# A hybrid decoder step on one core: the samples' and the prompt's softmaxes spread over the stick-breaking unit steps, and cache values in two passes

## The chip, the cores and the metric

One core of one Trainium2 chip runs the whole kernel. The metric is the device time of one execution in microseconds, the median of three runs.

## The reference

One layer of a decoder step, all in f32, for a prompt of 512 tokens and 8 samples with one new token each and 2048 cached positions in 16 pages of 128:

```python
h = rmsnorm(x, g_attn); z = h @ w_in            # 2840 columns
# stick-breaking heads (8), z = q k / 8, mask: key before query
log_1m = where(mask, log_sigmoid(-z), 0)
after  = reverse_cumsum(log_1m) - log_1m
o_sb   = where(mask, exp(log_sigmoid(z) + after), 0) @ v
# NSA heads (8 in 2 groups): compressed, selected (16 of 33 blocks), window
p_c = softmax(q kc); imp = sum over the group of p_c @ overlap; idx = top_k(imp, 16)
o_n = g0 * p_c vc + g1 * softmax(q k[idx]) v[idx] + g2 * softmax(window) v
x = x + [rmsnorm(o_sb), rmsnorm(o_n)] @ w_out
x = x + relu(rmsnorm(x) @ w_up)**2 @ w_down;  y = rmsnorm(x, g_final)
```

In the prompt all 8 selection blocks are within the 16 chosen, so the selected branch is plain causal attention; the block choice is computed for the samples alone. The caches are read by page id: keys and values of the stick-breaking cache (256 KB a page for each), of the selection cache (64 KB a page for each), the compression cache, and a window buffer.

## The kernel before

Each engine has one program in program order, joined by semaphores; `Chain` makes an instruction wait for the one before it on its own engine. SP issues the loads, one after the other. The stages in order of time are: input projection, loading and scoring of the cached keys with compression (until about 463 us), the prologue of the softmaxes, the unit steps, the output projection and the feed-forward part.

**Prologue** (462 to 534 us). PE (lines 807 to 877) and DVE (1729 to 1822) take turns, ACT fills in: `cp_qk`, `cp_max`, `cp_exp`, `cp_soft`, `cp_tr`, `cp_pT` are the prompt's compressed softmax, for four query tiles i, through banks 4 to 7 and `pbuf`; `row_max`, `row_max_diagonal`, `row_max_over`, `row_max_subtract`, `samples_exp`, `row_sum`, `row_sum_over`, `row_reciprocal` are the samples' window (0) and selected (1) softmaxes; `c_s` to `c_selm` the block choice (`rankA`, `rankB` compare 33 importances pairwise, in 1089 columns); `s_abs`, `s_sp`, `s_suf`, `s_c`, `s_d`, `s_a` the samples' stick-breaking logs, with `suf` summed over later pages by 15 chained additions.

**Unit steps** s = 0 to 47. Steps 0 to 15 are stick-breaking units m (head pair `pr`, key tile i = 3, 2, 1, 0, columns n = 128, 256, 384, 512, for two heads): `sb_qk` (PE), `sb_ln` (ACT, abs, exp, ln), `sb_soft` (DVE, three passes: sum, its rounded high part, its rounded low part), `sb_sum` (PE, high and low parts against `ntri` and `nones`, rounded matmuls), `sb_exp` (ACT), `sb_pv` (PE, two steps late). They use bank pairs 2 * (m % 3), so `sb_qk(m)` waits for the exponential of m - 3. Steps 16 to 47 are NSA units n = s - 16: `n_qk`, `n_max`, `n_exp`, `n_scale`, `n_tr` (one step late), `n_pT`, `n_pv` (two steps late), through banks 0 to 3, 4 and 5, 6.

**Cached values** ride in the steps on PE as `sample_values`, after `sb_qk` or `n_qk` and ahead of the value product: for a sample b, eight `page_pair` (four matmuls of 256 columns each, from the eight-slot `ring`), five `quad_values` (four matmuls of 128 columns, from five `quad` buffers), `last_values`. At a sample's end DVE's `acc_out` (line 1869) copies and clears bank 7, and PE's `gather_values` (985) waits for it. PAIRS and QUADS (lines 56, 57) lay this over six virtual steps a sample, 48 over steps 0 to 45. SP's loop (lines 555 to 568) issues, for each sample and half, four pages, four quad loads, four pages, four quad loads, and one window load a sample; every load waits for its buffer.

All matmuls of the steps that read plain f32 data are f32 and appear as two instructions each in the trace; the rounded ones (`fp32r` tiles) as one.

## Time and profile before

| | us |
|---|---|
| runs, median of 3 | 1224.68 (1223.98 to 1225.6) |
| the profiled execution | 1223.56 |
| its span | 1221.7 |
| mean granted TensorE clock | 0.919 of 2.4 GHz |

| engine | busy us | share of the span |
|---|---|---|
| PE | 1083.2 | 89% |
| DVE | 627.3 | 51% |
| ACT | 384.9 | 32% |
| POOL | 69.5 | 6% |

How to read it: the profile is one execution. PE is TensorE's matmuls, DVE VectorE, ACT ScalarE, POOL GpSimd, SP the engine that issues most DMAs; SPq is SP's queue in the act of issuing. A row of the timeline has start, length, engine, line, output <- input, shapes and, in brackets, the idle time before it and what ended it. The length of a matmul row contains the pipeline's latency, so two rows overlap a little; start to start is what it costs in a stream. `high_arena` and `low_arena` are the two halves of the on-chip memory, so most buffers carry these names.

### The profile page before, as it was taken

The numbers are of one execution on the slowest core, as the hardware profiler recorded it, in microseconds if no ns is written. First come the engines' busy times: TensorE is split into PE (matmuls) and PEld (weight loads), VectorE is DVE, ScalarE is ACT, GpSimd is POOL, SyncE is SP. The second block draws the span as 40 slices with busy tenths as digits, with TensorE's granted clock in tenths as the row PEclk, the third lists the DMA queues.
The fourth block names the chain that finished last, engine by engine and source line by source line (L and its number), as shares of the span: only waits on it lengthen the run. The fifth ranks groups of instructions, "written<-read, shape, count | busy, mean of one in ns | idle before, by whom it ended". The sixth has DMA issues, their size and how long they took to land.

```text
span 1221.7 us, 23078 instructions
## 1 busy us (share of the span) xinstructions
PE 1083.2 (89%) x8380; PEld 953.1 (78%) x8380; DVE 627.3 (51%) x1051; ACT 384.9 (32%) x710; POOL 69.5 (6%) x83
## 2 busy tenths in 40 slices
PE   3996997999988995479899998999999999999993
PEld 2995997888878885345555655999999999998993
DVE  4332665777877845744454556545552334553332
ACT  4111112333333321144454555332331112322223
POOL 2000002111111100000000000020000000000002
PEclk9998997988999875578898999999999999999997
DMA  7429228999999912025467774223332323332321
GB/s 253 163 87 206 76 77 224 254 256 265 264 262 267 259 47 87 0 94 176 145 209 237 228 243 155 70 70 88 101 103 85 88 88 85 100 88 87 87 70 70
DMA packets 180129, 177.59 MB, mean 145 GB/s; under 512 B 13063, under 2 KB 140676, under 8 KB 177700
## 3 DMA queue, kind: packets, MB, share of 16 engines
q1 hardware_dynamic: 178610, 171.33, 49.5%
q10 hardware_dynamic: 1458, 5.43, 1.4%
q8 instruction: 40, 0.66, 0.2%
q14 instruction: 21, 0.17, 0.1%
HBM read 170.83 MB, written 10.06 MB: 148 GB/s over the span
## 4 chain that ended last, share of the span: by engine, by line
PE 65%; SPq 15%; issue 6%; DVE 6%; DMA 4%; ACT 3%; POOL 0%; POOLq 0%; DVEq 0%; ACTq 0%
PE bank L621 61%; PE bank L625 4%; SPq L491 4%; SPq L530 3%; SPq L533 3%; DMA high_arena<-in_state_nsa_win_kv_dram 2%; SPq L484 1%; SPq L565 1%; SPq L560 1%; DMA low_arena<-in_cache_nsa_slc_kv_dram 1%; DMA high_arena<-in_w_in_dram 1%; DMA high_arena<-in_x_sample_dram 1%; ACT low_arena L1442 1%; SPq L497 0%; SPq L499 0%
## 5 line engine op out<-in xcount | busy, mean ns | idle before, releaser
L621 PE MATMUL bank<-high_arena 128*128 128x254 f32 (+8 forms) x1864 | 241.7, 349 | 9.6 <-ACT high_arena L1203 6.1
L621 PEld LDWEIGHTS bank<-high_arena 128*128 128x128 f32 (+4 forms) x1864 | 186.5, 153 | 48.4 <-ACT high_arena L1203 8.0
L1930 DVE TENSOR_TENSOR w_low<-high_arena,w_high 128x1024 fp32r<-128x1024 f32 x72 | 90.2, 1252 | 83.8 <-ACT w_high L1379 73.8
L625 PE MATMUL bank<-low_arena 128*128 128x128 f32 (+2 forms) x653 | 102.4, 299 | 34.5 <-DMA low_arena<-in_cache_nsa_slc_kv_dram 17.7
L625 PEld LDWEIGHTS bank<-low_arena 128*128 128x128 f32 (+2 forms) x653 | 82.5, 158 | 46.4 <-issue 28.7
L1379 ACT ACTIVATE w_high<-high_arena 128x1024 fp32r<-128x1024 f32 x72 | 76.4, 1060 | 115.1 <-PE bank L621 114.1
L621 PE MATMUL bank<-a_high,w_high 128*128 128x256 f32 (+1 forms) x512 | 104.2, 285 | 5.3 <-issue 2.9
L621 PE MATMUL bank<-h_high,w_high 128*128 128x256 f32 (+1 forms) x512 | 103.0, 282 | 1.8 <-DVE h_low L1957 1.8
L621 PE MATMUL bank<-a_low,w_high 128*128 128x256 f32 (+1 forms) x512 | 103.7, 284 | 0.0
L621 PE MATMUL bank<-a_high,w_low 128*128 128x256 f32 (+1 forms) x512 | 103.4, 283 | 0.0
L621 PE MATMUL bank<-h_low,w_high 128*128 128x256 f32 (+1 forms) x512 | 103.2, 283 | 0.0
L621 PE MATMUL bank<-h_high,w_low 128*128 128x256 f32 (+1 forms) x512 | 103.1, 283 | 0.0
L1654 DVE TENSOR_REDUCE low_arena<-low_arena 128x512 f32 x128 | 87.8, 686 | 18.3 <-DVE low_arena L1650 0.6
L621 PE MATMUL bank<-w_in_high,h_high 128*128 128x284 f32 x320 | 96.5, 302 | 0.8 <-issue 0.8
L1650 DVE TENSOR_TENSOR low_arena<-low_arena,high_arena 128x512 f32<-128x512 f32 x120 | 87.2, 726 | 19.2 <-DMA low_arena<-in_cache_sb_kv_dram 19.2
L621 PE MATMUL bank<-w_in_low,h_high 128*128 128x284 f32 x320 | 95.2, 297 | 0.0
L621 PE MATMUL bank<-w_in_high,h_low_in 128*128 128x284 f32 x320 | 95.1, 297 | 0.0
L621 PE MATMUL bank<-high_arena,low_arena 128*64 128x128 f32 (+6 forms) x636 | 76.1, 371 | 19.4 <-DMA high_arena<-in_w_in_dram 9.9
L621 PEld LDWEIGHTS bank<-a_high,w_high 128*128 128x128 f32 x512 | 79.9, 190 | 6.1 <-issue 5.9
L621 PEld LDWEIGHTS bank<-h_high,w_high 128*128 128x128 f32 x512 | 79.4, 188 | 2.0 <-issue 2.0
L621 PEld LDWEIGHTS bank<-a_high,w_low 128*128 128x128 f32 x512 | 80.0, 189 | 0.0
L621 PEld LDWEIGHTS bank<-a_low,w_high 128*128 128x128 f32 x512 | 79.9, 189 | 0.0
(224 smaller groups left out, 1585.9 us busy)
## 6 DMA issues: line engine op xcount, KB each, us to landing
low_arena<-in_cache_sb_kv_dram SPq DMA_DIRECT2D x128, 256.0 KB, 4.7
high_arena<-in_cache_sb_kv_dram SPq DMA_DIRECT2D x128, 256.0 KB, 3.7
high_arena<-in_cache_nsa_cmp_kv_dram SPq DMA_DIRECT2D x128, 128.0 KB, 5.0
high_arena<-in_w_up_dram SPq DMA_DIRECT2D x32, 512.0 KB, 4.1
high_arena<-in_w_down_dram SPq DMA_DIRECT2D x32, 512.0 KB, 4.2
high_arena<-in_w_in_dram SPq DMA_DIRECT2D x10, 1136.0 KB, 5.3
low_arena<-in_cache_nsa_slc_kv_dram SPq DMA_DIRECT2D x128, 64.0 KB
high_arena<-in_cache_nsa_slc_kv_dram SPq DMA_DIRECT2D x128, 64.0 KB, 2.9
```

The costliest lines, as they stand in the source:

```text
L484: return nc.values_load_multi_w_load_instructions(pt[0:1, ds(lo, 8)], engines=[mybir.EngineType.SP], min_val=0, max_val=NPHYS - 1, skip_ru ...
L491: sp.dma_start(nat[u][half][16 * p:16 * p + 16].rearrange("p t k h d -> p (t k h d)"), c_cmp[ds(pg, 1)].rearrange("o (c t) k h d -> (o c) ...
L530: sp.dma_start(kquad[n % 2][:, j], c_slc[ds(pages[p + j], 1), :, 0].rearrange("o s h d -> (o s) (h d)")).then_inc(sem(f"kq_in{n % 2}"), 16)
L533: sp.dma_start(kring[p], c_sb[ds(pages[p], 1), :, 0].rearrange("o s h d -> (o s) (h d)")).then_inc(sem(f"ring_in{p}"), 16)
L560: sp.dma_start(ring[:, u, :], c_sb[ds(pages[u], 1), :, 1].rearrange("o s h d -> (o s) (h d)")).then_inc(sem(f"ring_in{u}"), 16)
L565: sp.dma_start(quad[:, q, j, :], c_slc[ds(pages[u - 3 + j], 1), :, 1].rearrange("o s h d -> (o s) (h d)")).then_inc(sem(f"quad_in{q}"), 16)
L621: return T.matmul(out, lhsT=l, rhs=r, start=start, stop=stop, **k)
L625: return T.transpose(out, in_, ident[0:n, 0:n])
L1379: S.activation(w_hi_r[u], w_raw[u], ACT.Copy).then_inc(sem(f"w_hi{u}"), 1)
L1650: chain(V.tensor_tensor(k, k, qb[:, u, :], ALU.mult))
L1654: V.tensor_reduce(raw_scores(ds(i, 1), u)[:, p, :], k.rearrange("p (h d) -> p h d", h=H), AX.X, ALU.add).then_inc(sem(f"ring_free{p % 8}"), 1)
L1930: V.tensor_tensor(w_lo_r[u], w_raw[u], w_hi[u], ALU.subtract).then_inc(sem(f"w_lo{u}"), 1)
```

## The change

1. `sb_sum` and `sb_soft`: the sum over later keys uses plain f32 matmuls on one f32 tile `sp_tile`; the rounded high and low parts and DVE's two passes for them go. The order within the sum changes (diagonal first, then j from 3 down).
2. Stick-breaking units use two bank pairs (0 and 1, 2 and 3) instead of three; `sb_qk(m)` waits for the exponential of m - 2. Banks 4, 5 and 7 serve the small steps.
3. The prologue's work is cut into `small_steps(s)` and `small_steps_late(s)` and called in steps 0 to 13 on PE, DVE and ACT. Ahead of the steps there stay the samples' compressed scores, the gates and a few copies. `cp_qk` uses a block-diagonal key tile `kbd` (4 matmuls of 62 columns instead of 8 of 31), `cp_tr` goes half by half through bank 5.
4. `sample_values` comes at the end of PE's step (after the sum; in NSA steps after `n_pv` and ahead of `n_tr`). It starts with step 5. Pages come first, three, three and two pairs a step for samples 0 to 3, five steps a sample for 4 to 7 (steps 5 to 36); quads come in steps 19 to 45. Pages and quads of a sample end apart, so there are 15 ends (`VALUE_ENDS`: steps 7, 10, 13, 16, 21, 26, 29, 31, 36, 38, 39, 41, 42, 44, 45) with an `acc_out` and a `gather_values` each in the step after.
5. SP issues pages 0 (first half), quads 0, pages 0 (second half), pages 1 to 6, quads 1, pages 7, quads 2 to 7.
6. Buffers move to fit; `load_out(0)` waits for the NSA value product 24.

```diff
+def value_steps():
+    pairs, quads = [()] * (STEPS + 2), [()] * (STEPS + 2)
+    at = 5
+    for b in range(B):
+        m = 0
+        for n in ((3, 3, 2) if b < 4 else (2, 2, 1, 2, 1)):
+            pairs[at] = tuple((b, m + j) for j in range(n))
+            m, at = m + n, at + 1
+    b, q = 0, 0
+    for at, n in ((19, 1), (21, 1), (24, 1), (26, 1), (29, 1), (31, 1), (34, 2), (36, 2), (37, 3), (38, 2), (39, 5), (40, 3), (41, 2),
+                  (42, 5), (43, 3), (44, 2), (45, 5)):
+        quads[at] = tuple((b, q + j) for j in range(n))
+        b, q = (b + 1, 0) if q + n == 5 else (b, q + n)
...
+            load_pages(0, 0)
+            load_quads(0)
+            load_pages(0, 1)
+            with sp.Fori(1, B - 1) as b:
+                for half in range(2):
+                    load_pages(b, half)
+            load_quads(1)
+            for half in range(2):
+                load_pages(B - 1, half)
+            with sp.Fori(2, B) as b:
+                load_quads(b)
...
             def cp_qk(i):
+                if i == 0:
+                    pe.wait_ge(*signal("s_d", 1))
+                else:
+                    pe.wait_ge(sem("cp_pT"), 2 * i)
+                for g in range(G):
+                    ins = mm(bank[5][:, 2 * g * NCP:2 * (g + 1) * NCP], nqT[:, g, i * P:(i + 1) * P], kbd.rearrange("p k c -> p (k c)"))
                 ins.then_inc(sem("cp_qk"), 1)
...
+            def small_steps(s):
+                if s == 0:
+                    row_max(0)
+                if s == 1:
+                    scores_T()
+                    row_max_over(0)
+                if s == 3:
+                    weights_T()
+                if s == 4:
+                    importance()
+                if s in (5, 7, 9, 11):
+                    cp_qk((s - 5) // 2)
+                if s in (6, 8, 10, 12):
+                    cp_tr((s - 6) // 2, 0)
+                if s == 7:
+                    chosen_T()
+                if s == 8:
+                    chosen_mask()
+                if s == 9:
+                    row_sum_over(0)
+                if s == 10:
+                    row_max(1)
+                if s == 11:
+                    row_max_over(1)
+                if s == 13:
+                    row_sum_over(1)
...
             def sb_sum(m):
                 pr, i, n = sb_unit(m)
+                pe.wait_ge(sem("sb_sp"), m + 1)
+                for h in range(2):
+                    out = bank[2 * (m % 2) + h]
+                    ins = mm(out[:, 0:n], ntri, sp_tile(pr, i)[:, h], False, i == 3, skip_group_check=True)
+                    for j in range(3, i, -1):
+                        ins = mm(out[:, (j - i) * P:n], nones, sp_tile(pr, j)[:, h], False, j == i + 1, skip_group_check=True)
...
-                for v in sample_steps(s):
-                    sample_values(v)
+                small_steps(s)
                 if 2 <= s < SB_U + 2:
                     sb_pv(s - 2)
                 elif 2 <= s - SB_U:
                     n_pv(s - SB_U - 2)
                 if 1 <= s < SB_U + 1:
                     sb_sum(s - 1)
+                if s == 3:
+                    sample_sums()
+                if s in (6, 8, 10, 12):
+                    cp_tr((s - 6) // 2, 1)
+                sample_values(s)
...
+            def small_steps_late(s):
+                if s == 0:
+                    softplus_max()
+                if s == 1:
+                    later_pages()
+                if s == 3:
+                    sample_logs()
+                if s == 5:
+                    rank_equal()
+                if s in (5, 7, 9, 11):
+                    cp_soft((s - 5) // 2)
+                if s == 8:
+                    chosen_add()
...
             for s in range(STEPS):
                 n = s - SB_U
+                if s - 1 in VALUE_ENDS and n < 0:
+                    acc_out(VALUE_ENDS.index(s - 1))
+                small_steps(s)
                 if n < 0:
                     sb_soft(s)
                 else:
                     n_max(n)
+                small_steps_late(s)
+                if s - 1 in VALUE_ENDS and n >= 0:
+                    acc_out(VALUE_ENDS.index(s - 1))
```

In this diff `small_steps` is PE's, behind `sb_qk`, and `small_steps_late` DVE's, behind `sb_soft` or `n_max`. DVE's own `small_steps` holds, ahead of `sb_soft`: the diagonal (0), the compressed maximum and subtraction (1), `cmp_soft` and `row_sum(0)` (2), `cmp_groups` (3), the clear of bank 7 and `rank_greater` (4), `cp_max` (5, 7, 9, 11), `chosen_blocks` (7), `chosen_rows` (8), `row_max(1)` (9), its diagonal, subtraction, sum and reciprocal (10 to 13). ACT has `cp_exp` behind `sb_ln` of steps 5, 7, 9 and 11, and `cp_pT` in the steps after.

## Rows read from the trace of the kernel before

**Rows 1.** Stretches: busy us by engine (x instructions), granted clock, DMA share, GB/s.

```profile
462.00:534.00 72.00, 35.68 (x145) 26.13 (x146) 45.72 (x116) 12.70 (x25) 0.00 (x0) 0.52 0.12 37
534.00:622.00 88.00, 80.84 (x672) 49.61 (x672) 38.00 (x56) 46.88 (x64) 0.00 (x0) 0.89 0.56 174
622.00:694.00 72.00, 67.69 (x716) 40.46 (x714) 35.51 (x81) 35.08 (x95) 0.00 (x0) 0.95 0.71 222
694.00:741.00 47.00, 45.97 (x506) 27.39 (x502) 24.11 (x54) 23.88 (x64) 0.00 (x0) 1.00 0.79 244
```

**Rows 2.** Timeline of PE: start, length, what, idle before.

```profile
553.09 0.50 PE L621 MATMUL bank<-z_parts,ntri_r 128*128 128x512 f32 x1
...
555.34 0.51 PE L621 MATMUL bank<-z_parts,nones_r 128*128 128x384 f32 x3
...
556.97 1.08 PE L621 MATMUL bank<-high_arena,low_arena 128*64 128x512 f32 x4
...
586.54 1.13 PE L621 MATMUL bank<-low_arena 64*128 64x512 f32 x4
...
675.53 1.23 PE L621 MATMUL bank<-low_arena,high_arena 128*128 128x2 f32 x10
...
680.07 1.27 PE L621 MATMUL bank<-high_arena 128*8 128x256 f32 x24
...
693.16 1.09 PE L621 MATMUL bank<-high_arena,low_arena 128*64 128x128 f32 x16
...
740.15 1.09 PE L621 MATMUL bank<-high_arena,low_arena 128*64 128x128 f32 x16
```

**Rows 3.** Timeline of ACT in the stick-breaking steps.

```profile
588.08 1.03 ACT L1301 ACTIVATE high_arena<-bank 128x1024 f32<-128x1024 f32 x1 [0.83 <-PE bank L621]
...
590.23 1.15 ACT L1303 ACTIVATE high_arena<-high_arena,low_arena 128x1024 f32<-128x1024 f32 x1
...
622.16 1.02 ACT L1310 ACTIVATE high_arena<-bank 128x1024 f32<-128x1024 f32 x1 [5.39 <-PE bank L621]
```

**Rows 4.** Timeline of PE in the prologue, at half clock.

```profile
502.34 1.91 PE L625 MATMUL bank<-low_arena,high_arena 128*31 128x128 f32 x8 [3.87 <-DVE high_arena L1699]
...
523.48 6.68 PE L621 MATMUL bank<-high_arena,low_arena 128*128 128x512 f32 x8 [0.74 <-DVE low_arena L1725]
```

**Rows 5.** Timeline of DVE.

```profile
485.00 1.28 DVE L1772 TENSOR_TENSOR high_arena<-high_arena 16x1089 f32<-16x1089 f32 x1
...
493.73 3.85 DVE L1782 TENSOR_TENSOR high_arena<-high_arena 128x64 f32<-128x64 f32 x15
...
500.33 0.42 DVE L1693 TENSOR_TENSOR high_arena<-high_arena,low_arena 128x248 f32<-128x248 f32 x1
...
501.87 0.42 DVE L1699 TENSOR_TENSOR high_arena<-high_arena,low_arena 128x248 f32<-128x248 f32 x1
...
695.88 0.96 DVE L1849 TENSOR_REDUCE low_arena<-bank 128x2 f32<-128x768 f32 x1 [2.65 <-PE bank L621]
696.75 0.55 DVE L1874 COPY high_arena<-bank 128x384 f32<-128x384 f32 x1
```

**Rows 6.** Stretches of 4 us around a wait of PE for DVE.

```profile
592.00:596.00 4.00, 0.33 (x2) 0.33 (x2) 3.74 (x7) 1.27 (x4) 0.00 (x0) 0.80 0.00 0
596.00:600.00 4.00, 4.00 (x29) 2.61 (x29) 0.69 (x2) 0.00 (x0) 0.00 (x0) 0.50 0.00 0
```

**Rows 7.** Timeline of SP: DMA issues, merged.

```profile
697.96 2.86 SPq L565 DMA_DIRECT2D high_arena<-in_cache_nsa_slc_kv_dram  x4
...
701.74 3.08 SPq L560 DMA_DIRECT2D high_arena<-in_cache_sb_kv_dram  x4
...
711.32 0.44 SPq L568 DMA_DIRECT2D high_arena<-in_state_nsa_win_kv_dram  x1
...
713.21 1.92 SPq L560 DMA_DIRECT2D high_arena<-in_cache_sb_kv_dram  x4
```

**Rows 8.** Chain that ended last: a wait for a window load.

```profile
641.21 2.88 DMA high_arena<-in_state_nsa_win_kv_dram
```

More of the change, by code:

```diff
@@ L834, in row_sum_over @@
             def row_sum_over(br):
                 pe.wait_ge(*signal("m_sum", br + 1))
-                mm(bank[3][:, 0:64], ones, s64[:, 8, 64:128]).then_inc(sem("samples_pe"), 1)
-            for b in range(B):
-                ins = mm(bank[2][0:NC, b * H:(b + 1) * H], kc[:, b, 0:NC], qbd[:, b, :])
-            ins.then_inc(sem("samples_pe"), 1)
-            cp_qk(0)
-            row_max(0)
-            pe.wait_ge(*signal("c_s", 1))
-            tr(bank[2][0:64, 0:NC], s64[0:NC, 0, 0:64]).then_inc(sem("samples_pe"), 1)
@@ new lines, in chosen_T, with chosen_mask, sample_sums @@
+            def chosen_T():
+                pe.wait_ge(*signal("c_sel", 1))
+                tr(bank[4][0:NSEL, 0:16], s64[5][0:16, 0:NSEL]).then_inc(sem("samples_pe"), 1)
+            def chosen_mask():
+                pe.wait_ge(*signal("c_selx", 1))
+                mm(bank[4][:, 0:272], K("half")[0:NSEL, :], selx[0:NSEL].rearrange("p a b -> p (a b)")).then_inc(sem("samples_pe"), 1)
+            def sample_sums():
+                pe.wait_ge(*signal("s_suf", 1))
+                for c in range(2):
+                    out = bank[5 + 2 * c][:, 0:512]
+                    mm(out, ntri, sps[:, 4 * c:4 * c + 4].rearrange("p b n j -> p (b n j)"), True, False)
+                    ins = mm(out, nones, suf[:, 4 * c:4 * c + 4].rearrange("p b n j -> p (b n j)"), False, True)
+                ins.then_inc(sem("samples_pe"), 1)
@@ L1790, in _ @@
-            cp_soft(2)
-            dve.wait_ge(*signal("c_mask", 1))
-            V.tensor_scalar(selm.rearrange("p n k -> p (n k)"), bank[2][:, 0:272], -1.0, -NEG, ALU.add, ALU.mult).then_inc(sem("samples_dve"), 1)
-            dve.wait_ge(*signal("c_selm", 1))
-            for b in range(B):
-                v = slc[:, b].rearrange("p n (k g) -> p n k g", k=2)
-                chain(V.tensor_tensor(v, v, over(selm[:, :, 2 * b:2 * b + 2], 3, G), ALU.add))
-            row_max(1)
-            cp_max(3)
```

559 lines of the change are left out of this document (286 added, 273 removed).

## The prediction

> **What bounds the kernel now.** I read the stage table first [rows 1]. From 462 to 534 us stands the prologue that the change dissolves: PE is busy for 35.7 of 72 us at a granted clock of 0.52 (about its level of 1.2 GHz), DVE for 45.7. From 534 to 622 run the 16 stick-breaking unit steps, from 622 to 741 most of the NSA unit steps; PE is busy 81 of 88 us and 114 of 119 us there. So the prologue is bound by a chain over DVE and PE, the rest by PE. What lies before 462 and after 762 is not touched. What can be won is the prologue's idle time; what counts is where each wait goes.
>
> Durations at full clock, from the PE timeline [rows 2], start to start: the scores of a unit with 512 columns 1.1 us and 0.4 for their mask, its value product 1.0, its rounded sum matmuls from 553.09 to 555.8, 2.7 us; three page pairs 1.2 us, a gather of ten instructions 1.2 us. ACT takes 588.08 to 591.4 us for the three softplus passes of the widest unit and 1.02 us for its exponential [rows 3]. Over the four units of a head pair (128, 256, 384, 512 columns) scores make 4.4, value products 2.8, rounded sums 6.0 us.
>
> **Part 1: the sums in plain f32.** Removed: two of three DVE passes per unit (beside other work) and 40 rounded matmuls per head pair; added: 20 f32 ones. The only f32 row of that shape is eight instructions, four matmuls of 512 columns, in 6.68 us at half clock [rows 4]: 1.67 us each, 0.83 at full clock. A pair streams 256, 768, 1536 and 2560 columns in its four units, 5120 in all or ten such matmuls: 8.5 us with the small ones rounded up. So +2.5 us a pair, +10 us of PE. The widest unit's sum alone takes 4.3 us.
>
> **Part 2: the prologue in the steps.** PE work of steps 0 to 16: four pairs x (4.4 + 2.8 + 8.5) = 63; values of 32 page pairs x 0.4 = 13; compressed softmax 4 x (0.9 for scores, an estimate from half the instructions of before, + 0.95 for transposes, half of the 1.91 at half clock [rows 4]) = 7.5; the samples' sums 3.3; three gathers and the small ones 5: 92 us. The scores of step 0 can start at about 467 us, when the samples' compressed scores are out. Had PE never waited, step 16 would end at 559. It waits. I walked the steps with two bank pairs instead of three, so that scores of step s need the exponential of s-2:
> - Steps 0 to 4 have no page values to fill gaps and begin at half clock. DVE's 15 chained additions, 3.85 us [rows 5], the f32 sums and the samples' sums follow each other: exponential of step 3 at about 499.
> - Step 6: its first transposes wait for `cp_soft(0)`, which takes 2.0 us and is queued on DVE behind `rank_equal`, four operations of 1.28 us [rows 5]: PE idle about 6 us. Behind the wait in PE's queue stand the value product, the sum and the pages of the step. Its values end at 517.
> - Steps 8, 10 and 12 wait likewise for `cp_soft`: 0.7, 3 (behind `row_max(1)` too) and 1 us. Values of step 9 end at 538, of 12 at 563, of 16 at 584.
> - Three gathers 2 us, page loads that hold single steps 3 us, half clock after the stall of step 10 2 us: 591.
>
> Before, the same point (the last stick-breaking sum) is 622.1 [rows 3]. **Gain 31 us**, bounds 20 and 42. In it is that PE's waits on `acc_out`, behind one of which PE was idle for 3.7 of 4 us and then at half clock for the next 4 [rows 6], are gone, since `acc_out` now stands ahead of `sb_soft`.
>
> **Part 3: NSA steps 17 to 33.** Bare unit work is 10.0 us per four steps (scores 4.4, value products 2.8, transposes 2.8): 42.5, and the products with `vc` 3.2, together 45.7. Before, this stretch took 72 us (622.1 to 694.2 [rows 2]): besides these 12.6 of values, 3.7 of gathers, and stalls. After: 28 page pairs and six quads 12.5; gathers 4.3; `acc_out` now runs in the very step in which PE gathers, behind `n_max` (0.96 us, then a copy of 0.55 and a clear [rows 5]), less the value product that covers it: 1.5 us, five times, 7.5; the value product comes straight behind the scores and so ahead of ACT's copy, 2; oddments 1; and one wait on SP: `load_quads(1)` is queued ahead of `load_pages(7, 0)`, so from the pages of step 28 on SP needs 2 + 11.2 (part 4) + 1.4 + 2 us and the pages a landing, and step 32 waits about 4.5 us. The sum is 45.7 + 31.8 = 77.5 us, and step 33 ends at 668.5 against 694.2. **The gain is down to 26 us.**
>
> **Part 4: the second pass, and who issues it.** SP issues every one of these loads in order. Four DMAs take 1.92 us, 2.1 start to start; a new sample's page ids 1.45 us (711.76 to 713.21), those of its other half at least 0.92 (700.82 to 701.74) [rows 7]. One sample of quads is 17 DMAs: 1.45 + 4.2 + 0.92 + 4.2 + 0.45 = 11.2 us of SP with every buffer free. Before, a sample comes every 23 us, and SP hid this. Now the quads of six samples (2 to 7) are issued behind the last page load, which waits for the pages of step 33: the last issue starts at 668.5 + 2 + 67.2 - 0.5 and lands some 3.5 us later (2.9 in the shortest row of such a load [rows 8], more in a full queue): 741 us. Without that PE would reach it at 720: steps 34 to 45 hold 31 us of unit work, 10 of values, 2.6 of gathers and 8 of `acc_out` waits. So PE waits for SP, 21 us, in slices of 4 to 8 us at steps 39, 40, 42, 43 and 45. The step behind the last slice runs at half clock [rows 6]: the tail gets +2 us. Before, the matching point is 741.2, the end of the value product that now stands ahead of the last quads [rows 2]. **The gain is gone: 741 against 741.2.**
>
> Sum: the profiled execution's 1223.6 - 0.2 + 2; the runs' median lies 1.1 above it: **1226 us**. The forecast's own range is 1214 to 1240.
>
> **Rivals.**
> - **SP keeps up.** If an issue costs little in a light queue, step 45 comes at 720 and the time is 1226 - 21 = 1205. For it: the queue was busy in all rows of the second pass (244 GB/s in 694 to 741 [rows 1]), and these loads alone are a quarter of that. Against: four DMAs took 1.9 us whether of 256 or 64 KB each. The Trainium skill, DMA: Bandwidth & Descriptors, section Issuing engines are not separate DMA queues, says that the time in which a sequencer initiates a DMA is usually small relative to the DMA itself; by that rule the second pass isn't bound by SP, which is this rival. The trace speaks against the rule here, with 0.48 us of issue for 64 KB.
> - **The steps fill better than walked.** With full clock from step 2 on, step 16 ends at 580, and the time is 1215, since part 4 hangs on step 33 alone.
> - **Slower: the clock stays low.** The stalls of steps 6, 8, 10 and 12 come every 8 to 12 us. If they keep PE at 1.2 GHz through steps 0 to 13, some 45 us of matmul work that I walked at full clock doubles, and half of that falls into waits: +20, 1246. It decides if the mean granted clock from 500 to 560 is under 0.7. For it: the prologue stayed at 0.52 with PE half busy [rows 1]. The Trainium skill, TensorE: Matmul & The Clock Gate, Part 4: PE-mode transpose, says that transposes don't count as PE busy in the same way; by it the transposes of steps 6 to 12 don't help the clock, and the time would be this rival's.
> - **It doesn't do what it says:** the first waits of the steps (`c_s`, `m_diag`, `s_suf`) hold PE as the prologue did. DVE's work ahead of step 0 is 4 us; I count this within the low clock's case.
>
> **Chances.** Forecast case 0.60, of which 0.20 ends faster by over 0.2%, 0.14 within, 0.26 slower; SP keeps up 0.14; better steps 0.10; low clock 0.16. The bound of 0.2% (2.4 us) is about what a measurement of this kernel can tell from no change. Faster 0.44, within 0.14, slower 0.42. The range of 8 in 10 reaches from the first rival to the third: 1203 to 1246.
>
> **What would show it.** Right: the first stick-breaking exponential before 480 us; PE idle some 6 us in step 6, ended by DVE; the last stick-breaking exponential at 580 to 602; SP issuing without a gap from step 34 on, 11 us a sample; PE's longest waits of the last nine steps ended by loads into `quad`. Wrong: quads landed before PE asks; PE's waits on `acc_out` under 0.5 us; an NSA stage no longer than before; a granted clock under 0.7 or over 0.95 through the stick-breaking steps.

## The result: 0.9% slower, and the profile after

The changed kernel runs in 1234.97 us (median of 12, 1228.64 to 1246.17) against 1224.46 (median of 12) for the kernel before on the same chips: ratio 1.0087, 95% interval 1.0057 to 1.0116. Its profiled execution took 1234.02 us with a span of 1232.2, 10.5 more than before.

The stretches, cut as in [rows 1]: busy us by engine (x instructions), granted clock, DMA share, GB/s.

```profile
462.00:534.00 72.00, 62.40 (x333) 38.49 (x336) 37.73 (x96) 33.18 (x53) 0.00 (x0) 0.81 0.33 106
534.00:622.00 88.00, 80.75 (x660) 45.52 (x649) 39.72 (x80) 40.04 (x77) 0.00 (x0) 0.96 0.63 204
622.00:694.00 72.00, 66.41 (x628) 39.45 (x627) 29.85 (x70) 29.13 (x79) 0.00 (x0) 0.86 0.56 174
694.00:741.00 47.00, 36.23 (x347) 20.63 (x342) 13.91 (x37) 13.91 (x37) 0.00 (x0) 0.74 0.40 112
```

The first stretch is what the change meant it to be: PE busy 62 us instead of 36. The loss stands in the last: PE busy 36 of 47 us instead of 46, the clock down from 1.00 to 0.74, and the DMAs at 112 GB/s instead of 244, which speaks against the transfers as what PE waits for (experiments 1 and 2 settle it). The timeline of ACT (L1339 is the first mask copy, behind the last of the compression; L1361 `sb_exp`):

```profile
463.33 0.31 ACT L1285 ACTIVATE high_arena<-bank,high_arena 128x62 f32<-128x62 f32 x1 [6.38 <-PE bank L638]
...
465.71 0.31 ACT L1339 ACTIVATE ident_r<-low_arena 128x128 fp32r<-128x128 f32 x1 [1.40 <-DVE high_arena L1704]
...
476.20 0.36 ACT L1361 ACTIVATE high_arena<-bank 128x256 f32<-128x256 f32 x1
...
497.92 1.02 ACT L1361 ACTIVATE high_arena<-bank 128x1024 f32<-128x1024 f32 x1 [2.50 <-PE bank L638]
...
589.55 1.02 ACT L1361 ACTIVATE high_arena<-bank 128x1024 f32<-128x1024 f32 x1 [6.83 <-PE bank L638]
```

The first exponential comes at 476, the last at 589.55 instead of 622.16 [rows 3]: 32.6 us won. Then the timeline of PE:

```profile
510.16 1.06 PE L642 MATMUL bank<-low_arena,high_arena 128*31 128x128 f32 x4 [4.93 <-DVE high_arena L1760]
...
637.11 1.05 PE L638 MATMUL bank<-low_arena,high_arena 128*128 128x2 f32 x8 [1.46 <-DVE bank L2002]
...
642.97 1.90 PE L638 MATMUL bank<-high_arena 128*8 128x256 f32 x16
...
671.36 1.05 PE L638 MATMUL bank<-high_arena 128*8 128x256 f32 x16
...
746.21 0.61 PE L638 MATMUL bank<-high_arena 128*8 128x128 f32 x8 [2.45 <-DMA high_arena<-in_cache_nsa_slc_kv_dram]
...
749.78 1.55 PE L638 MATMUL bank<-high_arena 128*8 128x128 f32 x14 [1.02 <-DMA high_arena<-in_state_nsa_win_kv_dram]
...
774.16 0.51 PE L638 MATMUL bank<-mix_high,w_high 128*128 128x256 f32 x2 [2.88 <-DVE mix_low L2052]
```

510.16 is the transpose of step 6 that waits for `cp_soft(0)`. 637.11 is a gather waiting for `acc_out`, and 642.97 the pages of the next step at half clock: 1.90 us for sixteen instructions, where 671.36, the page values of step 33, has 1.05. The last quads wait for their loads and end at 751.3 (before: 741.2). The first product of the output projection starts at 774.16; before it started at 761.78. SP in that stretch:

```profile
675.05 10.64 SPq L570 DMA_DIRECT2D high_arena<-in_cache_nsa_slc_kv_dram  x16
...
725.64 9.02 SPq L570 DMA_DIRECT2D high_arena<-in_cache_nsa_slc_kv_dram  x16
734.85 0.44 SPq L573 DMA_DIRECT2D high_arena<-in_state_nsa_win_kv_dram  x1
736.75 9.89 SPq L570 DMA_DIRECT2D high_arena<-in_cache_nsa_slc_kv_dram  x16
746.83 0.45 SPq L573 DMA_DIRECT2D high_arena<-in_state_nsa_win_kv_dram  x1
```

A sample of quads is sixteen loads and a window load, 11.1 us from one sample to the next (725.64 to 736.75), with gaps only for the page ids. The chain that ended last (start, length) runs through these issues, 0.53 us from one to the next, and leaves SP only at the last window load:

```profile
713.48 0.34 SPq L570
714.01 0.33 SPq L570
...
721.63 1.40 SPq L570
...
742.62 0.34 SPq L570
...
746.83 2.91 DMA high_arena<-in_state_nsa_win_kv_dram
749.78 1.55 PE bank L638 x14
```

PE's waits on loads and on `acc_out` from 592 to 780, summed (us in total, times, longest):

```profile
PE bank L638 <- DMA high_arena<-in_cache_nsa_slc_kv_dram: 10.1, 7, 2.6
PE bank L638 <- DVE bank L2002: 8.6, 8, 1.5
PE bank L638 <- DMA high_arena<-in_state_nsa_win_kv_dram: 3.0, 3, 1.0
```

Quads' and window loads 13.1 us, `acc_out` 8.6 us.

**One table for all variants.** Parts of the program that none of them alters end at different times from one execution to the next: the first mask copy stands between 461.38 and 467.31. So each profile is measured from its own marks: A, the first mask copy; B, the exponential of step 3; C, the last stick-breaking exponential; D, the page values of step 33; E, the first product of the output projection. All differences are worked out from the timelines, in us; the ratios are of the timed runs to the kernel before.

| kernel | ratio (95%) | A to B | B to C | C to D | D to E | C to E |
|---|---|---|---|---|---|---|
| before | 1 | | | | | 139.6 |
| changed | 1.0087 (1.0057 to 1.0116) | 32.2 | 91.6 | 81.8 | 102.8 | 184.6 |
| changed, again | 1.0081 (1.0049 to 1.0114) | 32.2 | 91.1 | 81.4 | 105.7 | 187.1 |
| few issues | 0.9902 (0.9868 to 0.9936) | 36.3 | 92.1 | 80.1 | 80.0 | 160.1 |
| softmax first | 1.0103 (1.0069 to 1.0137) | 35.6 | 93.0 | 81.7 | 101.4 | 183.1 |
| sums copied first | 1.0036 (1.0016 to 1.0057) | 32.2 | 90.8 | 75.4 | 102.5 | 177.9 |
| two queues | 0.9969 (0.9946 to 0.9992) | 35.8 | 89.5 | 81.9 | 86.7 | 168.6 |
| even spread | 0.9853 (0.9828 to 0.9877) | 35.7 | 88.6 | | | 155.5 |
| together | 0.9829 (0.9797 to 0.9861) | 36.0 | 85.7 | | | 155.4 |
| spread, two queues | 0.9758 (0.9724 to 0.9792) | 35.9 | 85.2 | | | 145.4 |

**Where PE's time goes between the marks.** An estimate, worked out from the busy time and the granted clock of each microsecond of a stretch: idle is the time in which PE isn't busy; busy time multiplied by the granted clock is the work, in us at full clock; the rest of the busy time is what half clock cost. Values behind is the last kernel of experiment 8.

| stretch, kernel | us | idle | cost of half clock | work |
|---|---|---|---|---|
| A to C, before | 89.6 | 8.4 | 9.2 | 72.0 |
| A to C, f32 sums in the kernel before | 93.6 | 3.6 | 4.4 | 85.5 |
| A to C, two bank pairs in the kernel before | 102.8 | 18.8 | 11.6 | 72.4 |
| A to C, values behind | 89.4 | 10.6 | 8.5 | 70.3 |
| C to D, changed | 81.8 | 7.6 | 10.1 | 64.2 |
| C to D, changed, again | 81.4 | 11.2 | 5.5 | 64.7 |
| C to D, sums copied first | 75.4 | 7.8 | 2.9 | 64.7 |
| D to E, changed | 102.8 | 22.1 | 15.6 | 65.1 |
| D to E, few issues | 80.0 | 11.3 | 3.3 | 65.4 |
| D to E, two queues | 86.7 | 14.7 | 6.8 | 65.1 |
| C to E, before | 139.6 | 10.5 | 3.0 | 126.1 |
| C to E, values behind | 143.0 | 10.8 | 3.4 | 128.8 |
| C to E, even spread | 155.5 | 14.3 | 12.8 | 128.4 |
| C to E, together | 155.4 | 17.4 | 8.8 | 129.2 |
| C to E, spread, two queues | 145.4 | 10.7 | 5.6 | 129.0 |

The same stretch of the same program comes out at the same work to within about 1 us, whatever the idle time and the clock, so the division can be trusted to about that.

### The profile page after: what moved, and what is told of

The parts are those of the page before. It is cut to its first block, busy times and chain, and to the rows that moved or that the text cites. A ratio compares the mean times of both kernels' runs of the same rounds, so it can differ in the third digit from the quotient of the medians.

```text
span 1232.2 us, 23015 instructions
## 1 busy us (share of the span) xinstructions
PE 1108.8 (90%) x8348; PEld 960.3 (78%) x8348; DVE 606.1 (49%) x1032; ACT 383.7 (31%) x707; POOL 71.2 (6%) x83
## 4 chain that ended last, share of the span: by engine, by line
PE 66%; SPq 15%; issue 6%; DVE 5%; DMA 4%; ACT 3%; POOL 0%; POOLq 0%; DVEq 0%; ACTq 0%
PE bank L638 61%; PE bank L642 5%; SPq L492 4%; SPq L570 3%; SPq L531 3%; SPq L534 3%; DMA low_arena<-in_cache_nsa_slc_kv_dram 2%; SPq L485 2%; DMA high_arena<-in_w_in_dram 1%; DMA high_arena<-in_x_sample_dram 1%; DVE low_arena L1967 1%; ACT low_arena L1506 1%; ACT high_arena L1379 0%; DVE high_arena L2047 0%; SPq L498 0%
## 5 line engine op out<-in xcount | busy, mean ns | idle before, releaser
L638 PE MATMUL bank<-high_arena 128*128 128x254 f32 (+8 forms) x1864 | 247.6, 357 | 22.3 <-DMA high_arena<-in_cache_nsa_slc_kv_dram 10.1
L642 PE MATMUL bank<-low_arena 128*128 128x128 f32 (+3 forms) x658 | 112.2, 317 | 30.7 <-DMA page_ids<-in_page_table_dram 14.8
L642 PEld LDWEIGHTS bank<-low_arena 128*128 128x128 f32 (+3 forms) x658 | 91.2, 169 | 47.7 <-issue 32.7
L638 PE MATMUL bank<-high_arena,low_arena 128*64 128x128 f32 (+9 forms) x676 | 87.3, 372 | 15.9 <-DMA high_arena<-in_w_in_dram 8.8
L638 PE MATMUL bank<-low_arena 128*128 128x128 f32 (+9 forms) x366 | 80.4, 452 | 3.0 <-ACT high_arena L1361 2.9
L638 PEld LDWEIGHTS bank<-high_arena,low_arena 128*64 128x64 f32 (+2 forms) x676 | 47.8, 146 | 41.4 <-issue 27.5
```

Source lines behind the costliest of these rows:

```text
L638: return T.matmul(out, lhsT=l, rhs=r, start=start, stop=stop, **k)
L642: return T.transpose(out, in_, ident[0:n, 0:n])
```

## The experiments

**1. Is SP's issuing the pace of the second pass?** The same bytes by 5 issues a sample instead of 17. The kernel leaves out the page table there: it reads fixed pages, and so no page ids.

```diff
-                    for q in (2 * half, 2 * half + 1):
-                        sp.wait_ge(sem(f"vq_mm{q}"), b + 1)
-                        for j in range(4):
-                            sp.dma_start(quad[:, q, j, :], c_slc[ds(pages[4 * (q % 2) + j], 1), :, 1]...
+                for q in range(4):
+                    sp.wait_ge(sem(f"vq_mm{q}"), b + 1)
+                    sp.dma_start(quad[:, q], c_slc[4 * q:4 * q + 4, :, 1].rearrange("p s h d -> s p (h d)")).then_inc(..., 64)
```

> The changed kernel, with one part of SP's work taken away: for samples 2 to 7 each quad of the second pass comes by one load of four consecutive fixed pages (the same bytes) instead of four loads of one chosen page each, so SP issues 5 loads a sample instead of 17 and reads no page ids there. The selected branch of these samples therefore uses other pages than the page table names. Theory (SP's issues are the pace of the second pass): in the changed kernel windows of samples 2 to 7 were issued at 685.89, 699.21, 711.58, 723.75, 734.85 and 746.83, 12.2 us apart on average; with a third of the issues SP is never behind, the waits on quads' loads (10.1 us) go, TensorE's clock stays up through steps 37 to 45, the last values end at 735 to 741 instead of 751.3, and the time falls by 10 to 16 us, to 1219 to 1225. Rival (SP keeps up, and TensorE's own order with the buffers' release sets the pace): the spacing stays at 11 to 12 us, the waits go over to other names and the time stays at 1231 to 1236. Second rival (the bytes are the pace, 0.33 MB a sample): the waits on the quads' loads stay, as does the time.

Measured: 1212.81 us, a larger gain than was expected. D to E fell from 102.8 to 80.0 us, and C to D stayed within 2 us. SP's issues, and PE's waits on the quads' loads from 592 to 780:

```profile
712.60 3.23 SPq L567 DMA_DIRECT2D high_arena<-in_cache_nsa_slc_kv_dram  x4
716.03 0.41 SPq L569 DMA_DIRECT2D high_arena<-in_state_nsa_win_kv_dram  x1
718.58 3.75 SPq L567 DMA_DIRECT2D high_arena<-in_cache_nsa_slc_kv_dram  x4
722.52 0.41 SPq L569 DMA_DIRECT2D high_arena<-in_state_nsa_win_kv_dram  x1
```

```profile
PE bank L646 <- DMA high_arena<-in_cache_nsa_slc_kv_dram: 1.4, 3, 0.5
```

The last two windows are 6.5 us apart where they were 12.0 (734.85, 746.83), SP waits between its loads, and PE's waits on quads' loads are 1.4 us in all; the clock in 700 to 741 is 0.92 instead of 0.71. The DMAs move 190 GB/s there instead of 112, so the bytes weren't the pace. The pace was SP's issuing, page ids included. D to E fell by more than the waits on loads (13.1 us), because half clock went too: by the second table idle time fell by 10.8 us and the cost of half clock by 12.3, at the same work.

**2. The same loads from two engines.** Quads 2 and 3 of samples 2 to 7 are issued by GpSimd.

```diff
+            with pool.Fori(2, B) as b:
+                pages = ...            # page ids b * NPG + 8 and up, in GpSimd's registers
+                for q in (2, 3):
+                    pool.wait_ge(sem(f"vq_mm{q}"), b + 1)
+                    for j in range(4):
+                        G_.dma_start(quad[:, q, j, :], c_slc[ds(pages[4 * (q % 2) + j], 1), :, 1]...).then_inc(sem(f"quad_pool{q}"), 16)
```

> The changed kernel, with the loads of the second pass shared: quads 2 and 3 of samples 2 to 7 (8 loads a sample) are issued by GpSimd, which has nothing else to do there, quads 0 and 1 and the window (9 loads) by SP. Same loads, same buffers. Theory (the issues are the pace, not the transfers): SP needs 5.7 us a sample instead of 11.2; if GpSimd issues a load in 1 us or less the two together keep up, and the time is 1211 to 1220, near the version with few issues (1212.8). Rival 1 (a second issuing engine adds nothing): spacing of the windows still 11 to 12 us, 1231 to 1238. Rival 2 (GpSimd's issues cost more than 1.4 us each): it is the pace in SP's place, and the time is over 1235. The Trainium skill, DMA: Bandwidth & Descriptors, says that issuing from other engines does not add bandwidth; by that rule alone the first rival would follow.

Measured: 1221.38 us, 1.4 us above the theory's range; D to E 86.7 us. Neither the loads nor their bytes were changed here, only who issues them, so this is the clean form of experiment 1. GpSimd's issues, merged by four:

```profile
713.52 2.31 POOL L2178 DMA_DIRECT2D high_arena<-in_cache_nsa_slc_kv_dram  x4 [2.60 <-PE bank L645]
726.14 2.31 POOL L2178 DMA_DIRECT2D high_arena<-in_cache_nsa_slc_kv_dram  x4 [2.94 <-PE bank L645]
```

0.58 us an issue, beside SP's 0.53; in brackets, GpSimd waits for PE to free buffers, so it isn't the pace either. The Trainium skill, DMA: Bandwidth & Descriptors, section Issuing engines are not separate DMA queues, grants a second engine only the issue time, and calls that time usually small relative to the DMA itself. Here, moving 8 of the 17 issues of a sample took 16.1 us off D to E; the "usually" doesn't hold for loads of 64 KB that land a median 1.9 us after an issue of 0.53 us.

**3. VectorE's copy of the sums ahead of the row maxima.**

```diff
-                if s - 1 in VALUE_ENDS and n < 0:
+                if s - 1 in VALUE_ENDS:
                     acc_out(VALUE_ENDS.index(s - 1))
...
-                if s - 1 in VALUE_ENDS and n >= 0:
-                    acc_out(VALUE_ENDS.index(s - 1))
```

(and in `acc_out` a wait for the last quad of the step, if that step has one)

> The changed kernel, with VectorE's order alone changed: in the steps from 16 on it copies out and clears the samples' running sums (bank 7) ahead of the row maxima of the step instead of behind them. Theory: TensorE's eight waits of 8.6 us on that copy between 590 and 770 are gone (under 2 us left), and so are the stretches at half clock that begin behind five of them (the page values at 642.97, 653.75 and 664.84 took 1.90 us for 16 instead of 1.05); the page values of step 33 come 7 to 9 us earlier, counted from the last stick-breaking exponential (81.8 us behind it in the changed kernel). From there SP's issues set the pace and nothing comes back. Time 1226 to 1229. Rival (SP is the pace before step 33 as well, so that waits on page loads take the place of the copy's): less than 3 us earlier at step 33, time 1233 to 1236.

Measured: 1229.03 us; 6.4 us of C to D, D to E unchanged. The waits from 592 to 760:

```profile
PE bank L638 <- DMA high_arena<-in_cache_sb_kv_dram: 4.8, 2, 3.9
PE bank L638 <- DVE bank L2005: 0.7, 2, 0.4
```

The copy costs 0.7 us instead of 8.6, and 600 to 650 runs at a granted clock of 1.00 instead of 0.90. Its rival came in part: a new wait of 4.8 us on page loads (3.9 and 0.8) stands ahead of D. Taken off at its length, it leaves 70.6 us for C to D, and by that the five copies ahead of D, 5.6 us of waits, cost 11.2 us in the first profile of the changed kernel.

One profile can't fix that price, though. The second profile of the changed kernel (experiment 9) has the same five waits and 3.5 us on page loads besides, and its C to D is no longer; the same subtraction gives 7.3 us. The three variants with the same five waits (few issues, softmax first, two queues) give 7.4 to 9.1. What differs is the half clock behind the waits. C to D of the first and of the second profile (after the length come PE's busy time and, third from the end, the granted clock):

```profile
589.55:671.36 81.81, 74.25 (x666) 42.57 (x662) 35.05 (x82) 34.21 (x92) 0.00 (x0) 0.87 0.62 198
```

```profile
589.73:671.16 81.43, 70.21 (x666) 40.00 (x660) 35.06 (x83) 35.04 (x95) 0.00 (x0) 0.91 0.62 199
```

So these waits cost between 1.3 and 2 times their length. VectorE between 635.10 and 637.05 in the changed kernel shows why the copy was late: the maximum had to wait for the scores of its own step, and the copy for the maximum.

```profile
635.10 1.22 DVE L1967 TENSOR_REDUCE low_arena<-bank 128x2 f32<-128x1024 f32 x1 [0.82 <-PE bank L638]
636.24 0.41 DVE L2001 COPY high_arena<-bank 128x256 f32<-128x256 f32 x1
636.78 0.27 DVE L2002 MEMSET bank<- 128x256 f32 x1
```

**4. The softmax ahead of the ranking in step 5.** A miss.

```diff
-                if s == 5:
-                    rank_equal()
                 if s in (5, 7, 9, 11):
                     cp_soft((s - 5) // 2)
+                if s == 5:
+                    rank_equal()
```

> The changed kernel, with one swap: in step 5 VectorE finishes the prompt's first compressed softmax before it ranks the samples' blocks (five instructions, one of them 3.85 us long in the kernel before) instead of behind that. Theory: TensorE's wait of 5.3 us in step 6 falls to 1 us or less, the last stick-breaking exponential comes at 585 to 587 instead of 589.55, and, since nothing later than the second pass gives it back before step 33, the last values end 2 to 4 us earlier; time 1230 to 1233. Rival (the block choice is then late and its matmul in step 7 waits instead, or SP's second pass gives the gain back): the last exponential moves by less than 1.5 us, or it moves and the last values still end at 750 to 752; time 1234 to 1236.

Measured: 1237.23 us, no gain, and the last stick-breaking exponential at 594.53 instead of 585 to 587. The waits from 465 to 592:

```profile
PE bank L638 <- DVE high_arena L1961: 7.2, 2, 5.2
PE bank L642 <- DVE high_arena L1760: 0.3, 1, 0.3
```

The wait for the softmax fell from 5.3 us to 0.3, and one of 5.2 us for L1961, `sb_out(0)`, took its place (the waits for L1961 were 2.3 us in the changed kernel, now 7.2): that copy stood behind the ranking too, and the value product of the next head pair waits for it. Neither theory had named it. With both ahead of the ranking ("together" and "spread, two queues") B to C is 85.7 and 85.2 us, against 88.6 to 92.1 in the six profiles with neither.

**5. The even spread.** The cause of SP's rush is the order of the two passes, so the values are dealt out anew: from step 18 on, cycles of seven steps with the pages of one sample (1, 1, 1, 2, 1, 1, 1 pairs) and the quads of two (2, 2, 1, 0, 2, 2, 1), and SP's program in the order in which the steps release buffers.

```diff
-    for at, n in ((19, 1), (21, 1), (24, 1), (26, 1), (29, 1), (31, 1), (34, 2), (36, 2), (37, 3), (38, 2), (39, 5), ...
+    for c in range(4):
+        m, q = 0, 0
+        for k in range(7):
+            n = 2 if k == 3 else 1
+            pairs[18 + 7 * c + k] = tuple((4 + c, m + j) for j in range(n))
+            m += n
+            n = (2, 2, 1, 0, 2, 2, 1)[k]
+            quads[18 + 7 * c + k] = tuple((2 * c + (q + j) // 5, (q + j) % 5) for j in range(n))
+            q += n
```

> The changed kernel, with the samples' values dealt out anew from step 18 on: pages of samples 4 to 7 and quads of samples 0 to 7 in cycles of seven steps, each with one sample's eight page pairs and two samples' quads, and SP's loads written in the order in which those steps release the buffers. The same loads, the same matmuls, the last values in step 45 as before. Theory (six samples' quads in nine steps ask more issues of SP than it makes, while it idles before): SP needs about 0.57 us for each load with its page ids, 33 loads a sample, some 20.7 us for a page sample and a quad sample together and 32 us for a cycle of seven steps that lasts 37 to 39; no wait on quads' loads over 0.5 us, clock 0.95 or more in 700 to 741; the first product of the mix at 750 to 755 instead of 774.16, time 1209 to 1216. Rival (the loads' order in one queue now makes a late release of one kind hold up the other): waits on page loads of 10 us or more, time 1225 or more.

Measured: 1206.77 us, ratio 0.9853: faster than both kernels by doing the same work in another order, and faster than the theory's 1209 to 1216; the mix's first product comes at 742.34. The clock in 700 to 741 is 0.92, not the 0.95 named. PE's waits on quads' loads are gone from the list; on page loads there are 0.7 us left:

```profile
PE bank L673 <- DVE bank L2037: 4.9, 5, 1.7
PE bank L673 <- DMA high_arena<-in_cache_sb_kv_dram: 0.7, 2, 0.6
```

**6. All three together.**

> The even spread, with VectorE's copy of the sums ahead of the row maxima, and with the ranking of the samples' blocks in step 5 behind both the prompt's compressed softmax and the copy of the first head pair's output (the swap alone had moved TensorE's wait of 4.9 us from the softmax to that copy, 5.2 us). Theory: the three savings add, 8 us for the copy, 4 us for the ranking and 20 us for the spread; time 1199 to 1208, below the kernel before and below the version with few issues. Rival (the three are one another's cover, and TensorE's own work is the bound after the first): no more than 4 us below the even spread alone.

Measured: 1206.12 us, a ratio 0.0024 below the even spread's, inside their intervals. The time lies in the theory's range, but the three savings didn't add: the gain over the even spread is the rival's. B to C fell from 88.6 to 85.7 us, but C to E not at all (155.4). The waits say where VectorE's gain went:

```profile
PE bank L673 <- DMA high_arena<-in_cache_sb_kv_dram: 8.1, 4, 2.9
PE bank L673 <- DVE bank L2035: 0.9, 3, 0.6
```

From `acc_out` (4.9 us, now 0.9) to page loads (0.7, now 8.1), with 4.0 us less of half clock and 3.1 more of idle time: PE had caught up with the one queue. So the rival's reason, that TensorE's own work is the bound, isn't what the waits show, and experiment 7 tests it.

**7. The same with quads 2 and 3 issued by GpSimd.**

> The even spread with VectorE's two reorderings, and in it quads 2 and 3 of samples 2 to 7 issued by GpSimd instead of SP. Theory (with VectorE's waits gone TensorE has caught up with the one queue again: four waits of 8.1 us on page loads, three times behind eight quad issues of 4.0 us): SP has a quarter fewer issues in the cycles, the waits on page loads fall under 2 us, and the time falls by 4 to 8 us to 1198 to 1203. Rival (TensorE is the bound there, its clock falls or another wait comes in the place of these): under 2 us, 1204 to 1208.

Measured: 1197.62 us (1193.54 to 1202.83), ratio 0.9758, the best of the study: 2.4% under the kernel before, 3.3% under the changed one. It is 0.4 us under the theory's range; the rival, and with it TensorE's work as the bound, fell. Page waits from 592 to 760 are 0.9 us. C to E is 145.4 us: 6.7 us less idle time and 3.2 less half clock than together, at the same work. From 650 to 700:

```profile
650.00:700.00 50.00, 48.58 (x556) 29.64 (x554) 24.73 (x58) 24.18 (x64) 14.79 (x28) 1.00 0.83 246
```

**8. The two parts of the change that touch a step's own work, each alone in the kernel before.** Plain f32 sums, in one pass and one set of matmuls:

```diff
-                for low in range(2):
-                    pe.wait_ge(sem("sb_sp"), 2 * m + low + 1)
...
+                pe.wait_ge(sem("sb_sp"), m + 1)
+                for h in range(2):
+                    for j in range(i, NT):
+                        ins = mm(out[:, (j - i) * P:n], nones if j > i else ntri, sp_tile(pr, j)[:, h], False, j == NT - 1, ...)
```

> The kernel before, with one part of the change alone: the stick-breaking sums are kept and multiplied in plain float32, one VectorE pass and one set of matmuls for each step, instead of high and low parts in three passes with two sets. Theory (the forecast's first part): TensorE is the bound of steps 0 to 15 and four float32 sets cost it 2.5 us more for each head pair, 10 us in all; VectorE's saved passes are hidden. Last stick-breaking exponential at 630 to 632 instead of 622.2, time 1232 to 1234. Rival (the saved VectorE passes and their waits were on the path of each step): the last exponential stays within 2 us of 622 or comes earlier, and the time is 1218 to 1226.

Two bank pairs:

```diff
-                if m >= 3:
-                    pe.wait_ge(sem("sb_a"), m - 2)
+                if m >= 2:
+                    pe.wait_ge(sem("sb_a"), m - 1)
```

(and `m % 3` to `m % 2` throughout)

> The kernel before, with one part of the change alone: the stick-breaking steps turn over two pairs of PSUM banks instead of three, so that the scores of step m wait for the exponential of step m-2. Theory (the forecast's walk took no price for this beyond the waits that it named): the scores wait for ScalarE, which is 84% of a step behind, up to 1 us in a step; last exponential at 622 to 632 and time 1224 to 1234, most likely 1228. Rival (the third pair was what let TensorE run ahead in this kernel, whose sums wait for VectorE's three passes): 1 to 1.5 us in each of 16 steps, last exponential at 638 or later, time over 1238. Other rival: no price, 1223 to 1225.

And two pairs with the samples' values behind the sums, where the change has them:

```diff
-                for v in sample_steps(s):
-                    sample_values(v)
                 if 2 <= s < SB_U + 2:
                     sb_pv(s - 2)
...
                     sb_sum(s - 1)
+                for v in sample_steps(s):
+                    sample_values(v)
```

> The kernel before with two pairs of banks instead of three, and in each step the samples' values moved behind the sums of the step before (where the change has them) instead of ahead of them. Theory: the two pairs cost 12.9 us in 14 waits only because nothing stands between the sums of a step, with whose end ScalarE's exponential begins, and the scores that wait for it; with 1.2 us or more of values in between the wait is covered in most steps. Waits on the exponential under 4 us, last stick-breaking exponential within 90 to 94 us of the first mask copy (89.6 in the kernel before, 102.8 with two pairs alone), time 1224 to 1230. Rival (the order has nothing to do with it, the third pair is needed for running ahead): waits of 10 us and more stay, 1233 to 1240.

Measured: 1230.39 (ratio 1.0059, 1.0032 to 1.0085), 1236.34 (1.0103, 1.0068 to 1.0139) and 1232.12 us (1.0035, 1.0009 to 1.0062). From the first mask copy to C: 89.6 us in the kernel before, 93.6, 102.8 and 89.4. The last exponential of the three, and for the second and third PE's waits on the exponential (L1310) from 534 to 637:

```profile
621.66 1.02 ACT L1310 ACTIVATE high_arena<-bank 128x1024 f32<-128x1024 f32 x1 [7.22 <-PE bank L626]
```

```profile
635.96 1.02 ACT L1310 ACTIVATE high_arena<-bank 128x1024 f32<-128x1024 f32 x1 [6.36 <-PE bank L621]
PE bank L621 <- ACT high_arena L1310: 13.8, 15, 1.7
```

```profile
623.59 1.02 ACT L1310 ACTIVATE high_arena<-bank 128x1024 f32<-128x1024 f32 x1 [4.43 <-PE bank L621]
PE bank L621 <- ACT high_arena L1310: 5.9, 7, 1.7
```

**The sums** cost 4.0 us of the stage, not 10, and neither theory holds whole: the last exponential is where the rival had it, the time is above the rival's and below the theory's. The second table says how: PE's work rose by 13.5 us, more than the 10 of the forecast, but idle time fell by 4.8 us and the cost of half clock by 4.8. PE's waits for VectorE's clearing of the sums (L1875, L1866 in that kernel) fell from 6.5 us to 2.2. The 4.0 us are from one profile, the fastest of the six executions (1221.97 us); the timed runs say 7.2 us.

**Two pairs** alone cost 13.2 us of the stage, nearly all of it waits on the exponential, of which the kernel before has none in its list. The last exponential, 635.96, and the time lie between the theory's ranges and the rival's.

**With the values behind the sums** the stage is as long as before (89.4 us): the exponential starts at the end of the sums, and the values that follow cover part of the wait. But 5.9 us of waits are left, not under 4, and the time is above the theory's 1224 to 1230. Two other things help the stage. PE's waits for the clearing of the sums (6.5 us in the kernel before) are no longer in its list (4.3 us for `sb_out`, L1843, are new), and 1.7 us of work are no longer in the stage, because the last step's values now come behind mark C. That is most of what is lost behind C: of the 3.4 us there (C to E 143.0 instead of 139.6), 2.7 are work. From A to E two pairs with the values behind cost 3.2 us in the profile, and 4.3 us by the timed runs.

**9. The changed kernel again.**

> The changed kernel once more, unaltered, beside these. In its first profile TensorE's clock came up at 480, and in the profile of the version with the softmax first, whose instructions are the same up to step 4, only at 484, after which steps 0 to 3 took 3.8 us longer; and it had no wait on page loads at step 32, where three of its variants have one of 2 to 5 us. Theory (both are differences from one execution to the next, not of the variants): the time again 1230 to 1238, and in the profile at least one of the two is as in the variants: the clock up at 484 or a wait on page loads between 655 and 670. Rival (they belong to the variants): clock up at 480 counted from the same start and no such wait.

Measured: 1238.38 us. One of the two is as in the variants: there are 3.5 us of waits on page loads ahead of D. The clock again rose early (A to B 32.2 us). A third difference was not named: behind the wait on `acc_out` of 1.46 us at 637 the clock stood at half until 646 in the first profile and not at all in this one.

## Why the prediction was off by 9 us

The forecast was 1226 us, near the kernel before; the kernel took 1234.97, 10.5 us more than before. The direction was left open (0.44 for faster, 0.42 for slower), and the range was wide enough for both; the measured time lies in it. The forecast's mechanism, that the front is won and the second pass of quads gives it back because SP issues it, is shown by experiments 1 and 2. The sizes, step by step:

- **Start of the stage.** Forecast as in the profile before. The last step of compression is 2.3 us later (463.33 against 461.01), in code that is the same; over the nine profiles of the changed order mark A wanders by 6 us, so this can't be put down to the change.
- **Part 1, f32 sums, +10 us of PE.** Right in sign. In the kernel before they cost 4.0 us of the stage and 7.2 of the time (3.9 to 10.4 by the interval). PE's work itself rose by more than forecast, 13.5 us; what failed is that the forecast put nothing against it. It took VectorE's two saved passes as hidden, but idle time and half clock gave 9.6 us back, part of it in PE's waits for VectorE's clearing of the sums (6.5 us, then 2.2), so those passes were in part on PE's path.
- **Part 2, the walk.** By the clock it held to about 3.6 us: first exponential 476 (forecast before 480), exponential of step 3 at 497.9 (499), idle before the transposes of step 6 4.9 us (6), values of step 9 at 541.6 (538), of step 12 at 564.3 (563), last exponential 589.55 (591). Part of that is luck. The stage began 2.3 us late; PE's work from 467 to the end of step 16 was 99.2 us, not 92; and the waits for `cp_soft` in steps 8, 10 and 12 were 0.4 us in all, not 4.7, and those on page loads 1.5, not 3. The bank pairs cost 2.9 us of waits, in steps 2, 3 and 5, each behind a step without values; the walk had this right only in the changed order, as the 13.2 us of experiment 8 show.
- **Part 3, steps 17 to 33, 77.5 us.** Measured 81.9, from 590.5 to 672.4. The predicted wait on pages at step 32 isn't in the first profile, but is in the second (3.5 us) and in four variants. The waits on `acc_out` are 5.6 us (forecast 7.5). **What failed is the price of a wait**: it was taken as its own length. Work was priced well, 63.5 us with the oddments (45.7 + 12.5 + 4.3 + 1) against 64.2 measured, and idle time was 7.6 us instead of the forecast's 14. The 10.1 us that half clock cost are in no term of the sum: the clock stood at half for 3 to 7 us behind four of the five waits on `acc_out` (642.97 lies in such a stretch). The kernel before already showed this [rows 6], and the forecast applied it to the tail alone.
- **Part 4, the second pass.** 72.5 us forecast from the end of step 33 to the end of the last values, 78.9 measured: the largest miss. 11.2 us of SP a sample is right (11.1). The six samples begin 14.9, 11.2, 12.4, 12.2 and 11.1 us apart and take 72.2 us instead of 67.2. The forecast had every buffer free at each issue; SP waited 2.9 us for buffers, all of it up to the second sample's first load (689.96). Three later samples each hold one issue of 1.2 to 1.6 us where the others take 0.33 (721.63 in the chain above is one), and the profile names nothing that SP waited for there. On PE's side the waits on loads came as ten short ones of 13.1 us instead of five long ones of 21, and half clock, which the forecast left out ahead of the tail, cost 11.8 us between them. PE's work was 50.0 us, not 43.6 (31 + 10 + 2.6). SP's pace hid that miss; with few issues the stretch takes 57.0 us, where the forecast without SP has 51.5.
- **Tail +2.** Measured +2.3 (774.16 - 751.3 against 761.78 - 741.2). Behind it the profile after is 1.9 us shorter than before.

The misses are 2.3 + 1.6 (C and part 3 from the same start) + 6.4 + 0.3 - 1.9 = 8.7 us, which is the span's 1232.2 against the forecast's 1223.5.

**The rivals.** SP keeps up: fell with experiments 1 and 2; its price, 21 us, was the right size for what SP costs (22.8 us of D to E). The clock stays low: fell, it was 0.94 from 500 to 560. By the rule of the Trainium skill, TensorE: Matmul & The Clock Gate, Part 4: PE-mode transpose, that transposes don't count as PE busy in the same way, the transposes of steps 6 to 12 would not have helped; the trace doesn't speak against the rule, since there were matmuls enough around them. Better steps: within 2 us of the walk, not 11. The signs named for it came: first exponential before 480, SP at one sample every 11 to 15 us from step 34 on (without a wait only from the second sample on), most of the longest waits of the last steps on quads.

## What to carry to other kernels

Before work is gathered into one part of the schedule, count what else comes with it: here the matmuls of six samples fitted into nine steps, and their 102 DMA issues at 0.53 us and page ids didn't. The same wait of 1.5 us of TensorE was followed by 7 us of half clock in one profile and by none in another; the five waits on `acc_out` of C to D cost 1.3 to 2 times their length. So many short waits are worth the same search as one long one. Split a stretch into idle time, half clock and work before naming a cause; and ask of each wait what stands behind it on the engine that ends it, since the swap that frees one waiter holds up the next in that queue. And mend the limits in order: the reordering on VectorE gave nothing from C to E in experiment 6 until the queue behind it was relieved in experiment 7.

## What the runs showed of the hardware beyond that

- The clock's rise comes at two moments for the same instructions: in three of nine profiles of the changed order A to B is 32.2 us, in the other six 35.6 to 36.3. The granted clock in 480 to 488, of the changed kernel and then of the version with the softmax first, whose order up to there is the same:

```profile
480.00:484.00 4.00, 3.31 (x12) 2.08 (x10) 2.46 (x7) 2.14 (x3) 0.00 (x0) 0.68 0.46 133
484.00:488.00 4.00, 4.00 (x21) 2.75 (x20) 0.53 (x3) 3.23 (x3) 0.00 (x0) 1.00 0.00 0
```

```profile
480.00:484.00 4.00, 3.31 (x10) 2.41 (x11) 2.62 (x8) 2.33 (x3) 0.00 (x0) 0.50 0.49 144
484.00:488.00 4.00, 4.00 (x12) 1.58 (x9) 0.45 (x2) 1.99 (x2) 0.00 (x0) 0.50 0.01 4
```

  A single profile can't tell differences under 4 us here, the timed runs must.
- In experiment 2 GpSimd issued a 64 KB load in 0.58 us, nearly SP's 0.53, and its loads landed a median 2.5 us after the issue (SP's 2.2 beside them).
